# One core, two transformer stacks in fp32: the first projection in another order, and the experts' spread between gate and up

## The reference

```python
h = modulate(x, norm_mix, sh_m, sc_m)
(a_gate, a_x, q, kc, vc, ks, vs, kw, vw, gts) = _split(h @ w_in, IN0_SIZES)   # 512, 512, 512, 6 x 128, 24 columns
y_a = rg_lru(causal_conv(a_x, conv_w, conv_b), wa, ba, wx, bx, lam) * jax.nn.gelu(a_gate)
y_b = nsa_mixer(q, kc, vc, ks, vs, kw, vw, jax.nn.sigmoid(gts), ...)
x = x + g_m[:, None, :] * (jnp.concatenate([y_a, y_b], axis=-1) @ w_out)
# rg_lru: sigmoid gates r, i; a = exp(-8 r softplus(-lam)); h_t = a_t h_(t-1) + sqrt(1 - a^2) i x
# nsa_mixer: kc and vc are compressed: 15 blocks of 32 tokens, gelu(block @ w1) @ w2; q attends
#   to the compressed keys (softmax over 15), to selected blocks and to a window; gts weighs the three
```

```python
xs = jax.vmap(lambda hb, ib: hb[ib])(h, idx)
hid = jax.nn.silu(jnp.einsum('becd,edf->becf', xs, w_gate)) * jnp.einsum('becd,edf->becf', xs, w_up)
y = jnp.einsum('becf,efd->becd', hid, w_down) * g[..., None]
```

## Time and profile before

| what | us |
|---|---|
| runs: median (lowest to highest) of 3 | 1803.71 (1803.51 to 1804.05) |
| the profiled execution: its own time | 1802.05 |
| its span | 1800.3 |
| TensorE busy | 1645.6 (91%) |
| TensorE's weight loads busy | 1196.4 (66%) |
| VectorE busy | 714.0 (40%) |
| ScalarE busy | 323.8 (18%) |
| chain that ended last: TensorE, DMA, VectorE | 69%, 8%, 6% |

### The profile page before, as it was taken

The page is one execution under the profiler, slowest core; times in us unless marked ns, Lnnn a source line. Parts: engine busy times, 40 slices in busy tenths (PEclk is TensorE's granted clock), DMA queues, the critical chain, the costliest instruction groups (busy, mean ns, idle before and its releaser), DMA issues.

```text
span 1800.3 us, 22922 instructions
## 1 busy us (share of the span) xinstructions
PE 1645.6 (91%) x9755; PEld 1196.4 (66%) x9755; DVE 714.0 (40%) x1634; ACT 323.8 (18%) x773; POOL 79.8 (4%) x92
## 2 busy tenths in 40 slices
PE   6998999999998999999999999899998799996566
PEld 4784788888776888888778858745354585852112
DVE  2223367777327287776332242302022424221102
ACT  3031410000215200000232232310000323210000
POOL 0001400000005000000001020000000002000000
PEclk9986999999999999999999999899999999998888
DMA  9637479985762656785334325099997532689996
GB/s 361 223 109 247 172 268 357 340 330 210 256 171 95 234 188 233 281 301 207 118 113 155 137 98 234 1 402 409 409 409 284 187 127 118 263 319 409 409 409 267
DMA packets 168537, 443.72 MB, mean 246 GB/s; under 512 B 7754, under 2 KB 21236, under 8 KB 168436
## 3 DMA queue, kind: packets, MB, share of 16 engines
q1 hardware_dynamic: 168068, 442.13, 66.0%
q10 hardware_dynamic: 368, 0.13, 0.0%
HBM read 441.20 MB, written 1.05 MB: 246 GB/s over the span
## 4 chain that ended last, share of the span: by engine, by line
PE 69%; DMA 8%; DVE 6%; issue 3%; ACT 2%; POOL 2%; PEld 1%; PEldq 1%; ACTq 0%; DVEq 0%; SPq 0%
PE bank L666 67%; DMA scr<-in_w_up 4%; DMA ring<-in_w_gate 3%; PE bank L677 2%; POOL scr L1887 2%; DMA ring<-in_w_down 1%; PEld bank L666 1%; DVE scr L1935 1%; PE bank L722 1%; DVE xT L2466 1%; DVE scr L2337 0%; DVE scr L1943 0%; PEldq L1500 0%; ACT scr L1622 0%; ACT scr L1559 0%
## 5 line engine op out<-in xcount | busy, mean ns | idle before, releaser
L666 PE MATMUL bank<-hT,ring 128*128 128x256 f32 (+1 forms) x2576 | 499.2, 382 | 3.8 <-ACT hT L1567 3.8
L666 PEld LDWEIGHTS bank<-hT,ring 128*128 128x128 f32 (+1 forms) x2576 | 408.6, 177 | 91.7 <-issue 17.4
L666 PE MATMUL bank<-scr,ring 128*128 128x256 f32 (+3 forms) x1604 | 353.3, 380 | 10.9 <-DVEq L2305 5.8
L666 PEld LDWEIGHTS bank<-scr,ring 128*128 128x128 f32 (+2 forms) x1604 | 290.3, 190 | 60.7 <-issue 14.2
L2001 DVE SCALAR_TENSOR_TENSOR scr<-scr,csil 128x512 f32<-128x512 f32 x420 | 290.9, 747 | 3.2
L666 PE MATMUL bank<-scr 128*32 128x512 f32 (+8 forms) x1504 | 208.5, 433 | 14.9 <-issue 3.6
L666 PEld LDWEIGHTS bank<-scr 128*32 128x32 f32 (+4 forms) x1504 | 131.0, 159 | 88.5 <-issue 66.2
L666 PE MATMUL bank<-ring,scr 128*32 128x512 f32 (+2 forms) x1344 | 164.7, 603 | 11.6 <-DMA ring<-in_w_down 7.4
L1887 POOL TENSOR_SCALAR scr<-scr,small 128x256 f32<-128x256 f32 (+2 forms) x88 | 79.7, 922 | 1446.5 <-DVE small L2051 1270.1
L666 PEld LDWEIGHTS bank<-ring,scr 128*32 128x32 f32 (+2 forms) x1344 | 59.9, 116 | 106.4 <-issue 91.0
L2474 DVE TENSOR_TENSOR brow<-brow,bank 128x512 f32<-128x512 f32 x12 | 7.9, 685 | 243.3 <-ACT brow L1855 243.3
(11 more groups left out here) (246 smaller groups left out, 1143.8 us busy)
## 6 DMA issues: line engine op xcount, KB each, us to landing
ring<-in_w_gate SPq DMA_DIRECT2D x25, 2048.0 KB, 19.0
ring<-in_w_down SPq DMA_DIRECT2D x25, 2048.0 KB, 23.8
scr<-in_w_ada SPq DMA_DIRECT2D x23, 2048.0 KB, 9.1
scr<-in_w_up SPq DMA_DIRECT2D x21, 2048.0 KB, 23.6
scr<-in_l_mod_w SPq DMA_DIRECT2D x14, 2048.0 KB, 16.2
ring<-in_w_up SPq DMA_DIRECT2D x11, 2048.0 KB, 15.5
ring<-in_l_mod_w SPq DMA_DIRECT2D x10, 2048.0 KB, 9.4
ring<-in_l_ffn_wg SPq DMA_DIRECT2D x10, 2048.0 KB, 13.0
```

The costliest lines, as they stand in the source:

```text
L666: ins = nc.tensor.matmul(out, lhsT, rhs, start=start, stop=stop, skip_group_check=True)
```

## The change

**Order.** The pieces come as in0-1 (a_x), in0-3 (kc, vc, ks, vs), lru, cmp, in0-2 (q), in0-0 (a_gate), in0-4 (gates, kw, vw), then the six modulation pieces.

**Short between long.** The 16 compression products of the keys stand two by two between the 8 products of ks, those of the values between the 16 of vs, and the gates' 16 products between the 8 of kw. The lru products follow vs; the `w2` products stand after the third part of q, the scores after the third and fourth part of a_gate; two modulation pieces stand before the turn of `pc`, four behind it.

**ScalarE and VectorE** take the jobs in the new order. The gelu of the compression stands after ks; exp and tanh of the recurrence before the copies of q; its square root after them; then gelu of a_gate, exp of the scores, sigmoid of the gates, kw, vw. VectorE does both score halves before it waits, multiplies the recurrence's result with a_gate's gelu after them, and holds two sets of sums.

**Experts.** `spread(g-1)` and `turn_weights(g)` stand between the gate and the up products; VectorE does `weigh(g)` and `add_spread(g-1)` before the product with up; ScalarE copies the turned weights before its silu.

```diff
     out = list(ADA_AT["start"])
-    out += [("in0", s) for s in (1, 0, 2, 3, 4)]
-    out += [("lru",), ("cmp",)] + ADA_AT["lru"]
+    out += [("in0", 1), ("in0", 3), ("lru",), ("cmp",), ("in0", 2), ("in0", 0), ("in0", 4)] + ADA_AT["lru"]
...
+            wl = use(("lru",))
+            wc = use(("cmp",)).rearrange("p (i c n) -> p i c n", i=2, c=CMP_STRIDE)
+            wax = wl[:, 0:512].rearrange("p (i a j) -> p i a j", i=2, a=LC)
+
+            def compress(kv, first, end):
+                for c in range(first, end):
+                    mm(cmp_bank[:, kv * 32:kv * 32 + 2 * NBLK], wc[:, kv, c, :],
+                       ft[kv][:, c].rearrange("p g b -> p (g b)"), start=(c == 0),
+                       stop=(c == CMP_STRIDE - 1), signal=pe_to_act if kv and c == CMP_STRIDE - 1 else None)
+
             b = bank_for_act()
-            to_T(b[:, 0:T], w, 256, P, signal=pe_to_act)
+            cmp_bank = bank_for_act()
+            pe.wait_ge(dve_made_for_pe, n["from_dve"] + LC + 1)
+            for c in range(DC):
+                mm(b[:, 0:T], w[:, c, 256:256 + P], hT[:, c, :], start=(c == 0), stop=(c == DC - 1),
+                   signal=pe_to_act if c == DC - 1 else None)
+                compress(0, 2 * c, 2 * c + 2)
+            pe.wait_ge(dve_made_for_pe, n["from_dve"] + LC + 2)
             b = bank_for_act()
-            for t in range(NT):
-                to_tok(b[:, t * P:(t + 1) * P], w, 384, P, t, signal=pe_to_act if t else None)
+            for c in range(DC):
+                compress(1, 2 * c, 2 * c + 2)
+                for t in range(NT):
+                    mm(b[:, t * P:(t + 1) * P], hT[:, c, t * P:(t + 1) * P], w[:, c, 384:384 + P],
+                       start=(c == 0 and t == 0), stop=(c == DC - 1), signal=pe_to_act if t and c == DC - 1 else None)
             release()
-            w = use(("in0", 4))[:, 0:DC * 280].rearrange("p (c n) -> p c n", c=DC)
-            b = bank_for_act()
-            to_T(b[:, 0:T], w, 0, P, signal=pe_to_act)
-            b = bank_for_act()
-            for t in range(NT):
-                to_tok(b[:, t * P:(t + 1) * P], w, 128, P, t, signal=pe_to_act if t else None)
-            b = bank_for_act()
-            for t in range(NT):
-                to_tok(b[:, t * 24:(t + 1) * 24], w, 256, 24, t, signal=pe_to_act if t else None)
-            release()
-            wl = use(("lru",))
-            wax = wl[:, 0:512].rearrange("p (i a j) -> p i a j", i=2, a=LC)
             for m in range(LC):
                 b = bank_for_act()
                 from_dve()
...
-                       h1[:, 1, g, :], w2[:, 1, :],
-                       signal=pe_to_dve if j == 3 and g else None)
-            for _ in range(2):
-                release()
-
-            from_dve()
+            w = use(("in0", 2)).rearrange("p (c n) -> p c n", c=DC)
+            for m in range(4):
+                b = bank_for_act()
+                to_T_halves(b[:, 0:T], (w, w), (m * HD, 256 + m * HD), pe_to_act)
+                if m == 2:
+                    from_act()
+                    b = bank_for_dve()
+                    for g in range(2):
+                        mm(b[g * HD:(g + 1) * HD, 0:NBLK], w2[:, 0, :], h1[:, 0, g, :])
+                    for j in range(4):
+                        for g in range(2):
+                            mm(b[32 * j:32 * j + NBLK, 64 + g * HD:64 + (g + 1) * HD],
+                               h1[:, 1, g, :], w2[:, 1, :],
+                               signal=pe_to_dve if j == 3 and g else None)
+                    for _ in range(2):
+                        release()
+            release()
+            w = use(("in0", 0)).rearrange("p (c n) -> p c n", c=DC)
+            for m in range(LC):
+                b = bank_for_act()
+                to_T(b[:, 0:T], w, m * P, P, signal=pe_to_act)
+                if m >= 2:
+                    if m == 2:
+                        from_dve()
+                        pe.wait_ge(act_read, n["act"] - m - 1)
+                    t = m - 2
+                    for g in range(2):
+                        b = bank_for_dve()
+                        mm(b[:, 0:P], ident, cmp_mask[:, t, 0:P], start=True, stop=False)
+                        for c in range(4):
+                            mm(b[:, c * 32:c * 32 + NBLK], q0[g * HD:(g + 1) * HD, c, t * P:(t + 1) * P],
+                               kc[g * HD:(g + 1) * HD, 0:NBLK], start=False, stop=True,
+                               signal=pe_to_dve if c == 3 else None)
+            release()
+            w = use(("in0", 4))[:, 0:DC * 280].rearrange("p (c n) -> p c n", c=DC)
+            bg, b = bank_for_act(), bank_for_act()
+            for c in range(DC):
+                for t in range(NT):
+                    mm(bg[:, t * 24:(t + 1) * 24], hT[:, c, t * P:(t + 1) * P], w[:, c, 256:280],
+                       start=(c == 0 and t == 0), stop=(c == DC - 1), signal=pe_to_act if t and c == DC - 1 else None)
+                mm(b[:, 0:T], w[:, c, 0:P], hT[:, c, :], start=(c == 0), stop=(c == DC - 1),
+                   signal=pe_to_act if c == DC - 1 else None)
+            b = bank_for_act()
             for t in range(NT):
-                for g in range(2):
-                    b = bank_for_dve()
-                    mm(b[:, 0:P], ident, cmp_mask[:, t, 0:P], start=True, stop=False)
-                    for c in range(4):
-                        mm(b[:, c * 32:c * 32 + NBLK], q0[g * HD:(g + 1) * HD, c, t * P:(t + 1) * P],
-                           kc[g * HD:(g + 1) * HD, 0:NBLK], start=False, stop=True,
-                           signal=pe_to_dve if c == 3 else None)
+                to_tok(b[:, t * P:(t + 1) * P], w, 128, P, t, signal=pe_to_act if t else None)
+            release()
+            ada_pieces(ADA_AT["lru"][0:2], False)
             for t in range(NT):
                 b = bank_for_dve()
                 from_dve()
@@ -1111,6 +1129,7 @@
                     turn(b[:, i * P:(i + 1) * P],
                          pc[:, t, 4 * i:4 * i + 4, :].rearrange("p a b -> p (a b)"),
                          pe_to_dve if i else None)
...
                                         mm(banks[2 * s + kind][32 * j:32 * j + 32, :],
                                            xs[s][:, c, 32 * j:32 * j + 32], w[:, j, c2, :], start=(c == 0),
                                            stop=(c == DC - 1), signal=slots_released if last else None)
+                        if kind == 0:
+
+                            if g:
+                                spread(g - 1)
+                            turn_weights(g)
                     pe.drain().then_inc(gu_done, 1)
-                    if g:
-                        spread(g - 1)
                     if g < NG - 1:
                         gather(g + 1)
-                    turn_weights(g)
                     for i, s in enumerate(streams):
...
-                link(nc.vector.reciprocal(sm8, sm8))
-                link(tt(sm8, sm8, gts[:, t, :, 0], ALU.mult))
-                tt(pc[:, t], pc[:, t], bc(sm8, 2, [P, 8, 32]), ALU.mult).then_inc(dve_made_for_pe, 1)
+                link(nc.vector.tensor_reduce(sm8[t], pc[:, t], X, ALU.add))
+                link(ts_(sm8[t], sm8[t], 1e-30, None, ALU.max))
+                link(nc.vector.reciprocal(sm8[t], sm8[t]))
+            dve.wait_ge(act_read, gates_written[0])
+            for t in range(NT):
+                link(tt(sm8[t], sm8[t], gts[:, t, :, 0], ALU.mult))
+                tt(pc[:, t], pc[:, t], bc(sm8[t], 2, [P, 8, 32]), ALU.mult).then_inc(dve_made_for_pe, 1)
             for t in range(NT):
                 b = job()
...
                             ins.then_inc(spread_added, 1)
 
                 n["moe_bank"] += 2 * ns
+                dve.drain().then_inc(dve_chain, 1)
+                n["chain"] += 1
+                dve.wait_ge(dve_chain, n["chain"])
                 for g in range(NG):
+                    weigh(g)
+                    if g:
+                        add_spread(g - 1)
+                    n["moe_bank"] += ns
                     for i, s in enumerate(streams):
                         dve.wait_ge(hid_silu, halves_ + g * ns + i + 1)
                         tt(hid[s], hid[s], banks[2 * s + 1][:, :], ALU.mult).then_inc(hid_ready, 1)
-                    if g:
-                        add_spread(g - 1)
-                    weigh(g)
```

83 lines of the change are left out of this document (31 added, 52 removed).

## The result

The changed kernel takes 1786.38 us (median of 4 runs, 1784.74 to 1787.01), the kernel before beside it 1803.61 (1799.58 to 1804.05): ratio 0.9912, 95% interval 0.9893 to 0.9932. Forecast: 1785.0. A second measurement gave 1782.29 (5 runs, 1779.50 to 1787.26) against 1804.34, ratio 0.9884 (0.9862 to 0.9905). The profiled execution took 1784.74 with a span of 1783.0, against 1802.05 and 1800.3: 17.3 us less.

A forecast was written before the change was run, and what follows sets the result against it. TensorE was taken as the bound (1645.6 of 1800.3 us busy), DMA in layer 1's experts. Terms -3.2 - 2.3 - 10.9 - 3.6 + 1.1 = -18.9 gave a median of 1784.8, stated as 1785; range 1780 to 1790, with rivals 1777 to 1794.

The forecast's parts named there:

- Compression: First stage: its 64 loads, set beside ks and vs, stay at full clock and take 7.04 us: -3.2 us.
- Rival B: Short products' loads run further ahead: ks with its compression half takes 5.3 us, not 7.0; -3.4, total 1781.4; chance 0.12.
- w2 and scores: First stage: w2 some 0.5 us at full clock (-2.3); four score blocks 5.1, VectorE waits hidden (-10.9).
- The cover: TensorE's long work beside recurrence and softmax (13.8 and 16 us) hides their waits; without it up to 5 us return.
- New waits: Around lru and q, from ScalarE's sigmoid table load: 0.9, 0.2 and 0.1 us; priced +1.1, could be 0 to 3.
- Modulation pieces: End of the first stage: six pieces at full clock take 19.2 us instead of 22.7: -3.6.
- rival C: The cover doesn't hold: last modulation piece or the probabilities come late; +3 to +8 us, total 1790; chance 0.09.
- Attention: Its first product moves from 169.95 to about 151 us; later than 156 would make the prediction wrong.
- The clock: First stage: clock at 1.00 from 68 to 150 us, since no stretch is made of short products alone.
- A: The clock falls all the same in the first stage: costs 2 to 5 us, total 1788.5; chance 0.13.
- Experts: Layer 0: moved spread and turns give 0 (-1 to +2); layer 1 ends with its last landing, 0 (-2 to +3).
- D: Experts starve: up pieces released later, DMA queue runs dry, 35 us lost, total 1820; chance 0.04.

The follow-up runs named there:

- experiment 8: Changed kernel with the four score blocks behind vw, the turns directly behind them and all six modulation pieces last: 1794.97 us (one run).
- experiment 5: Changed kernel with the four lru products moved behind q's first part and the sigmoid table loaded ahead of q's first copy: 1788.78 us, ratio 0.9926.
- experiment 1: Changed kernel with the experts put back as in the kernel before, so the new order of the first projection alone: 1792.39 us, ratio 0.9928.
- experiment 3: Changed kernel with the short compression and gates products in blocks instead of mixed between long ones: 1792.34 us, ratio 0.9952.
- experiment 6: Changed kernel with the gates made within vw's products, one product of 152 columns for both: 1782.96 us, ratio 0.9894.
- experiment 7: Changed kernel with both lru behind q's first part and the gates within vw's products: 1780.87 us, ratio 0.9878.
- experiment 10: Changed kernel with lru behind q's first part, gates within vw's products, and scores one by one between a_gate's long products: 1782.60 us, ratio 0.9882.
- experiment 2: Kernel before with the experts' part of the change alone: 1804.87 us, ratio 1.0005.
- experiment 11: Kernel before with six slots instead of nine in the ring of the experts' layer 0: 1812.91 us, ratio 1.0044.
- experiment 4: Kernel before in its old order, with only the compression set two by two between kw's and vw's products: 1810.12 us, ratio 1.0044.
- experiment 12: Kernel before with the experts' part of the change and six slots in the experts' layer 0: 1811.57 us, ratio 1.0042.

## Why the prediction was right, point by point

**Compression, forecast 7.04 us beside ks and vs.** ks, vs and the 32 products take 14.72 us (68.02 to 82.74), of which 0.19 is a wait. Without the wait and without ks and vs, which took 7.13 in the kernel before (95.75 to 102.88), the compression takes 7.4. A ks product with its two short ones takes 0.88 us, which is 0.43 and four loads of 0.11, so ks as a whole 7.0. Rival B said 5.3 and is refuted. It leant on the Trainium skill, "TensorE: Matmul & The Clock Gate", section "Step-by-step: what each phase is for", on loads that are pulled ahead of matmuls in flight; in the trace the loads do run ahead, the short product's by 0.21 us (68.35 against 68.56), but with two short products behind a long one nothing beyond the sum is saved by it.

**w2 and scores, forecast 0.5 and 5.1.** Measured 0.57 (97.92 to 98.49), and 2.71 for two score blocks (112.56 to 115.27), 5.4 for four. The cover holds with room: recurrence and softmax come without a wait. That its loss costs "up to 5 us" was measured as 4.83 (experiment 8); that it then costs some 4 us more by the clock was not in the prediction.

**New waits, forecast 0.9, 0.2 and 0.1.** 0.74 before lru's third part and 0.17 before q's first came as said. The 0.2 before lru's first part did not; a wait of 0.19 stands instead before the values' compression, for ScalarE's copy of ks (L1674), which the sum didn't have. So the 1.10 in all agree with the forecast by luck in part. In experiment 5 the first wait is gone, with the table loaded earlier and lru moved.

**Modulation pieces, forecast 19.2 plus the turns.** From vw's end (132.45) to the attention 19.73, with turns of 0.56: 19.17. None of them waits for its transfer: rival C did not occur.

**Attention, forecast 151.06, measured 152.18.** The 1.1 us are terms that were each sized a little low: the compression 7.4 instead of 7.04, the score blocks 0.3, vw 3.78 instead of 3.6, gates with kw 7.13 instead of 7.0, q and three parts of a_gate 24.5 (87.53 to 112.56 without `w2`) instead of 24.2.

**The clock, "likely full, since no stretch is made of short ones alone".** This is the step whose reason failed. That the profiled execution came out right is luck: with the same order the clock fell in experiments 1 and 5. Mixing does keep the clock in the compression (experiment 3 against all others). But the score blocks behind a_gate's third and fourth part stayed blocks, of short and 64-row products. Seven traces have them there, and in five of them (experiments 1, 3, 5, 6 and 7) the clock fell near the end of the last block or up to 2 us behind it, whether gates in a block, gates with kw, or kw alone followed. In experiment 8, without scores there, it stayed full through the gates with kw and fell at the scores; in 10, with the scores mixed, it stayed full. So the scores are the likely cause, though 8 and 10 are one trace each, and the clock can also hold by chance. Where it falls, kw alone brings it back in about 3.5 us (experiments 6, 7), and gates with kw do not: it came back only within vw, 13 and 17 us after the fall (1, 5). I priced A at 2 to 5 us. From the start of the last score block to the attention the changed kernel takes 31.63 us (120.55 to 152.18), experiment 1 takes 38.18 (119.54 to 157.72) and experiment 5 takes 39.83 (119.53 to 159.36), so the fall costs 6.6 and 8.2. A's 0.13 was too low as well. Scores are not the only products that do it: in the old order the clock fell behind the gates' block in two of four traces (experiments 2 and 11).

The Trainium skill, "TensorE: Matmul & The Clock Gate", section "HAM oscillation — how this bites in real kernels", has the clock fall through idle gaps of TensorE. Experiment 4 agrees, where the clock fell within the wait of 8.82 us. These traces show falls without a gap too: 0.66 with PE and PEld both busy 10.00 of 10.00 us (experiment 3).

**Experts, forecast 0 (-1 to +2) and layer 1's end 0 (-2 to +3).** +0.07 in layer 0, and 194.91 against 194.96 behind layer 1's first product. Alone, 1.0005. D did not occur with nine slots, nor at six, where its own arithmetic said it had to show.

**The end follows.** -17.8 at the attention, -17.4 at the first expert product (1165.94 to 1148.57), -17.3 at the end. That the median came within 1.4 us of the forecast is partly luck, since the stretch behind the attention alone varies by 5 us from trace to trace.

## What to carry to other kernels

Short products cost nearly the same in a block and between long ones of the same row count; what they cost beside themselves is the clock of everything behind them. So set them between long ones, but not 64-row products between 128-row ones, which cost more here than the clock gave back. Keep long work for TensorE behind every chain that goes through other engines. Where a product shares its stationary tile with another, widen it rather than place it well. Price a clock fall at the length of all that follows until long products bring it back, and give it a chance of its own even where a first trace is clean.

## What the runs showed of the hardware

- The granted clock can fall or hold in the same stretch of the same products: 1.00, 0.66, 0.57 and 1.00 from 112 to 116 us in four traces of the old order (kernel before, experiments 2, 11, 12), 1.00, 1.00, 0.53 and 0.50 from 122 to 130 us in four of the new one (changed kernel twice, experiments 1, 5).
- It can fall with TensorE busy throughout (experiment 3) as well as in a wait (experiment 4).
- 64-row products set between 128-row ones take 0.95 us a pair where the two apart take 0.68, and their weight loads are not run ahead of them. Between products that both use 128 rows nothing is lost (0.88 for one long and two short, 0.87 by their parts).
- 24 more moving columns in 32 instructions of 128 cost 0.5 us, 16 products of 24 columns by themselves 3.7 (7.13 for gates and kw less 3.46).
